# A float32 Hymba-style decoder block on one core: the last pass's rows fetched ahead of a scatter, the end of the program in another order, the first loads on two queues, and unread products in TensorE's waits

## The reference, cut to what matters

```python
h = _rmsnorm(x, norm1_g)
z = h @ w_in                      # u_ssm | q | 6 k/v parts | gates
y_ssm = _s5_mixer(u_ssm, ...)     # 32 groups of 16 channels, 64 complex states, scan over tokens, GELU, GLU
y_attn = _nsa_mixer(q, ...)       # compressed, selected and window attention, mixed by gates
x = x + concatenate([y_ssm, y_attn]) @ w_out
h = _rmsnorm(x, norm2_g)
x = x + _hier_moe(h, ...)         # 4 groups of 8 experts; top-1 group, top-2 experts in it, gated MLP of width 256
return _rmsnorm(x, final_g)
```

## Time and profile before

| | |
|---|---|
| median of 3 runs | 1100.4 us |
| the profiled execution | 1097.68 us |
| its span | 1095.8 us |
| granted TensorE clock, mean | 0.956 |
| PE busy | 1001.9 us (91%) |
| DVE busy | 487.8 us (45%) |
| ACT busy | 279.9 us (26%) |
| POOL busy | 152.5 us (14%) |

### The profile page before, as it was taken

One profiled execution on the slowest core, in us unless ns is written; L12 is line 12 of the kernel. 1 busy time (PEld: TensorE's weight loads), 2 busy tenths in 40 slices (PEclk: granted clock), 3 DMA queues, 4 the chain that ended last, 5 costly groups with the idle time before them and its releaser, 6 DMA issues. The chain is left out here.

```text
span 1095.8 us, 13448 instructions
## 1 busy us (share of the span) xinstructions
PE 1001.9 (91%) x5091; PEld 588.6 (54%) x5091; DVE 487.8 (45%) x1212; ACT 279.9 (26%) x630; POOL 152.5 (14%) x147
## 2 busy tenths in 40 slices
PE   6999999986799999999999999996999889899882
PEld 4434677765565466766667455564454334444431
DVE  3477661049635456665665224264732111112115
ACT  3200011130222376666655011020101000001133
POOL 4000000032201221211010000011121111211231
PEclk9999999997899989999999999996999989999986
DMA  9201020042500190000000232546789999999964
GB/s 258 99 1 45 1 77 1 1 44 78 97 1 0 33 280 3 1 1 2 1 2 1 77 144 106 211 159 240 290 308 352 366 410 396 394 390 385 348 201 172
DMA packets 53345, 163.70 MB, mean 149 GB/s; under 512 B 24347, under 2 KB 26459, under 8 KB 40919
## 3 DMA queue, kind: packets, MB, share of 16 engines
q1 hardware_dynamic: 45184, 144.42, 36.4%
q0 software_dynamic: 8096, 18.42, 6.6%
HBM read 145.31 MB, written 25.24 MB: 156 GB/s over the span
## 5 line engine op out<-in xcount | busy, mean ns | idle before, releaser
L1932 PE MATMUL banks<-shared,wout 128*64 128x512 f32 (+1 forms) x416 | 148.9, 624 | 10.3 <-issue 8.6
L1540 PE MATMUL banks<-wout,shared 128*128 128x512 f32 x256 | 112.7, 594 | 0.5 <-PEq L1200 0.5
L368 PE MATMUL banks<-x,wout 128*128 128x512 f32 x256 | 112.0, 594 | 1.1 <-DVE x L409 1.1
L1932 PEld LDWEIGHTS banks<-shared,wout 128*64 128x64 f32 (+1 forms) x416 | 56.8, 168 | 83.0 <-issue 82.6
L1248 ACT ACTIVATE shared<-shared,low 128x640 f32<-128x640 f32 (+7 forms) x128 | 92.9, 729 | 3.0 <-DVE low L1335 2.5
L1980 DVE SCALAR_TENSOR_TENSOR mix_bt<-mix_bt,slot_coef,banks 128x256 f32<-128x256 f32 x24 | 11.5, 480 | 171.1 <-ACT mix_bt L1960 171.1
L1298 PE MATMUL banks<-consts,shared 128*128 128x128 f32 x528 | 79.2, 286 | 1.9 <-ACT shared L1248 1.1
L1954 PE MATMUL banks<-shared,hidt 128*64 128x512 f32 (+1 forms) x208 | 75.3, 611 | 5.9 <-issue 4.6
L368 PEld LDWEIGHTS banks<-x,wout 128*128 128x128 f32 x256 | 47.8, 190 | 60.2 <-issue 58.1
L1298 PEld LDWEIGHTS banks<-consts,shared 128*128 128x128 f32 x528 | 56.9, 142 | 41.6 <-issue 36.7
L1540 PEld LDWEIGHTS banks<-wout,shared 128*128 128x128 f32 x256 | 47.6, 190 | 55.2 <-issue 55.2
(11 more groups left out here) (362 smaller groups left out, 1264.9 us busy)
## 6 DMA issues: line engine op xcount, KB each, us to landing
shared<-in_exp_w_down SPq DMA_DIRECT2D x26, 1024.0 KB, 18.2
shared<-in_exp_w_gate SPq DMA_DIRECT2D x26, 1024.0 KB, 16.9
shared<-in_exp_w_up SPq DMA_DIRECT2D x26, 1024.0 KB, 21.5
x<-in_exp_w_gate SPq DMA_DIRECT2D x6, 1024.0 KB, 15.6
x<-in_exp_w_up SPq DMA_DIRECT2D x6, 1024.0 KB, 23.2
x<-in_exp_w_down SPq DMA_DIRECT2D x6, 1024.0 KB, 24.2
shared<-in_x SPq DMA_DIRECT2D x8, 512.0 KB, 7.7
wout<-in_w_in SPq DMA_DIRECT2D x2, 2048.0 KB, 8.4
```

The lines of the kernel that those rows point to most:

```text
L368: ins = nc.tensor.matmul(bank[:], slot[:, c, c0:c0 + P], ht[:, c, half * 512:half * 512 + 512], **flags)
L1540: ins = nc.tensor.matmul(psum[n % 4], src[:, i * P:i * P + P], m["wout"][:, k, half * 512:half * 512 + 512], start=k == 0, stop=k == KD - 1)
L1932: ins = nc.tensor.matmul(psum[2 + p][rows].rearrange("p (a f) -> p a f", a=2), xt[:, p, k, rows], wgu[b][:, :, k], start=k == 0, stop=k == ...
```

## The change

The first loads: x's tile 0 and the gain are issued by ACT, each on a semaphore of its own, the constants and tiles 1 to 3 by SP. PE and ACT wait for tile 0 alone, then for tile 1. A new helper, `keep_warm`, issues products of the identity with 512 columns of the constants into a bank that nobody reads: 7 ahead of the wait for m3, 7, 14 and 6 among the waits of the state-space stage, and 11 ahead of the wait for pass 0's rows. In the state-space stage the wait for `products` moves from the third round to the second, and `own(4)` to `own(7)` are spread over rounds 1 to 3. At the end, gather 23 moves ahead of a scatter, and ACT's, DVE's and SP's lists take another order; tiles 0 and 1 are now the shared ones.

```diff
@@ stage_project
+    def x_landed(eng, i):
+        if i < 2:
+            eng.wait_ge(x_in[0] if i else x_first, 16)
+        else:
+            eng.wait_ge(x_in[i // 2], 32)
...
-            sp.dma_start(x_tile[0], x_view[0]).then_inc(x_in[0], 16)
             sp.dma_start(m["consts"][:], d["consts"]).then_inc(consts_in, 16)
-            sp.dma_start(g1[:], d["norm1_g"][0].rearrange("(p k) -> p k", k=KD)).then_inc(consts_in, 16)
-            for i in range(1, 4):
-                sp.dma_start(x_tile[i], x_view[i]).then_inc(x_in[i // 2], 16)
+            sp.dma_start(x_tile[1], x_view[1]).then_inc(x_in[0], 16)
+            for i in (2, 3):
+                sp.dma_start(x_tile[i], x_view[i]).then_inc(x_in[1], 16)
...
+            act.dma_start(x_tile[0], x_view[0]).then_inc(x_first, 16)
+            act.dma_start(g1[:], d["norm1_g"][0].rearrange("(p k) -> p k", k=KD)).then_inc(g_in, 16)
             for i in range(4):
                 square(i)
...
@@ stage_s5
+            keep_warm(nc, m, psum[0], 7)
             pe.wait_ge(m3_in, 16 * 2 * STEPS)
...
             for n in range(4):
-                if n == 2:
+                if n == 1:
                     pe.wait_ge(products, 16)
-                    for later in range(4, 8):
-                        own(later)
+                    own(4)
+                    own(5)
+                    keep_warm(nc, m, psum[7], 7)
+                elif n == 2:
+                    own(6)
+                    keep_warm(nc, m, psum[7], 14)
+                elif n == 3:
+                    keep_warm(nc, m, psum[7], 6)
+                    own(7)
                 pe.wait_ge(turned, n + 1)
...
+def keep_warm(nc, m, bank, count):
+
+    for _ in range(count):
+        nc.tensor.matmul(bank, m["ident"], m["consts"][:, 0:512], start=True, stop=True)
...
@@ stage_moe
-    by_norm = [("x", i) for i in (0, 1, 5, 6, 7)] + [("z", i) for i in range(DIRECT)]
-    shared_tiles = (2, 3, 4)
-    store_order = (0, 1, 2, 5, 3, 6, 4, 7)
+    by_norm = [("x", i) for i in range(2, NT)] + [("z", i) for i in range(DIRECT)]
+    shared_tiles = (0, 1)
+    store_order = (2, 3, 4, 0, 5, 1, 6, 7)
...
-                    gp.wait_ge(s["x_t"], 2 * (n + 2 - UN) + 2)
-                    gather(n + 2)
+                    for ahead in ((n + 2, n + 3) if n + 4 == NP else (n + 2,) if n + 4 < NP else ()):
+                        gp.wait_ge(s["x_t"], 2 * (ahead - UN) + 2)
+                        gather(ahead)
...
             act_gate(act, first, first % 2)
-            squares((0, 1, 2, 3))
+            squares((0,))
             act_gate(act, first + 1, (first + 1) % 2)
             act_hid(act, first, first % 2)
+            squares((1, 2, 3))
+            act_hid(act, first + 1, (first + 1) % 2)
             act_roots(act, groups[0], 4)
-            squares((4, 5))
-            act_hid(act, first + 1, (first + 1) % 2)
-            squares((6, 7))
+            squares((4, 5, 6, 7))
             act_roots(act, groups[1], 8)
-            scaled_tile(2, ("x", 0))
             squares((8, 9))
             act_roots(act, groups[2], 10)
-            scaled_tile(3, ("x", 0))
-            scaled_tile(4, ("x", 5))
+            for i in shared_tiles:
+                scaled_tile(i, ("x", 2))
...
+            keep_warm(nc, m, psum[7], 11)
             pe.wait_ge(x_in[0], 16)
...
             dve.wait_ge(fg_in, 16)
+            dve_sum(dve, first)
             inverses(0)
-            dve_scaled(("x", 0))
-            dve_sum(dve, first)
-            dve_scaled(("x", 1))
+            for i in (2, 3):
+                dve_scaled(("x", i))
+            dve_sum(dve, first + 1)
             inverses(1)
-            dve_sum(dve, first + 1)
-            for i in (5, 6, 7):
+            for i in (4, 5, 6, 7):
                 dve_scaled(("x", i))
             inverses(2)
```

More of the change, by code:

```diff
@@ L194, in stage_project @@
     count = {kind: [sum(job[0] == kind for job in jobs[:k + 1]) for k in range(len(jobs))] for kind in "ft"}
+    x_first, g_in = sem("x_first_in"), sem("norm1_g_in")
+    def x_landed(eng, i):
[3 more added lines that the diff above has]
+            eng.wait_ge(x_in[i // 2], 32)
     with nc.Block() as block:
@@ L245, in square @@
             def square(i):
-                act.wait_ge(x_in[i // 2], 32)
+                x_landed(act, i)
                 if i >= 2:
@@ L258, in scale_row @@
                 nc.scalar.copy(scale[:, h * 512:h * 512 + 512], psum[3]).then_inc(scale_out, 1)
+            act.dma_start(x_tile[0], x_view[0]).then_inc(x_first, 16)
+            act.dma_start(g1[:], d["norm1_g"][0].rearrange("(p k) -> p k", k=KD)).then_inc(g_in, 16)
             for i in range(4):
                 square(i)
-            act.wait_ge(consts_in, 32)
+            act.wait_ge(consts_in, 16)
             roots(0)
@@ L305, in x_transposes @@
             def x_transposes(i):
-                pe.wait_ge(x_in[i // 2], 32)
+                x_landed(pe, i)
                 for half in range(2):
@@ L375, in job @@
                 ins.then_inc(mm_done, 1)
-            pe.wait_ge(consts_in, 32)
+            pe.wait_ge(consts_in, 16)
             for i in range(4):
@@ L434, in _ @@
             V.memset(tabx[BUCKETS:BUCKETS + 1], MASKED).then_inc(masked_in, 1)
-            dve.wait_ge(consts_in, 32)
+            dve.wait_ge(consts_in, 16)
+            dve.wait_ge(g_in, 16)
             for i in range(4):
@@ L1848, in stage_moe @@
     junk = m["first_rows"][:].rearrange("p b i q -> p b (i q)")
-    last_in = [(t, 48) for t in m["tiles_in"]] + [(t, 16 * n + 16) for t, n in zip(m["x_stored"] + m["xn_stored"][:1], (4, 2, 2, 4))]
+    last_in = [(t, 48 if k else 32) for k, t in enumerate(m["tiles_in"])] + [(t, 16 * n + 16) for t, n in zip(m["x_stored"] + m["xn_stored"][:1], (4, 2, 2, 4))]
     ss_done, root_done, o_done, out_stored = sem("ss3_done"), sem("root3_done"), sem("o_done3"), sem("out_stored")
```

## The result

The changed kernel takes 1110.37 us (median of 4, 1108.55 to 1111.11), the kernel before, timed beside it, 1100.4 (its three undisturbed runs; a fourth took 1495.32 and is left out): a ratio of 1.0091, 95% interval 1.0073 to 1.011. It is slower by about 10 us, 0.9%. The prediction had 1109.5, in a range of 1103 to 1115. The profiled execution is 1108.55 us with a span of 1106.6; against the span of before, 1095.8, that is +10.8.

A forecast was written before the change was run, and what follows sets the result against it. The prediction took PE's list as the bound, with DVE setting the state-space stage until the fill lengthens PE's list. Terms -1.2 + 15.9 + 3.2 - 8.8 = +9.1 gave 1109.5 us against the median, range 1103 to 1115.

The forecast's parts named there:

- The price of an unread product: All fill batches: one unread product shows as two entries of 0.43 us, so costs 0.86 us at full clock.
- State-space stage, +15.9: State-space stage: fill lengthens PE's list, round 3 ends 17.4 us later, transposes gain 1.5; +15.9 us, bounds +14 to +18.
- Router to first pass, +3.2: Ahead of pass 0: eleven unread products end 5.9 us behind the rows' landing, part given back by faster work; +3.2 us.
- some 4 us in: Eleven unread products ahead of pass 0: the clock rises some 4 us into the batch, which ends at 759.9.
- near 762: Sign to look for: the first gate-and-up product starts near 762, at the full clock.
- some 7 us in, +6: Upper bound of the router-to-first-pass term: were the clock to rise some 7 us in, it would be +6 us.
- Start, -1.2: Kernel start: tile 0 goes at once, so job(0) starts at 14.5 instead of 15.78; -1.2 us, none to -2.5.
- about 0.5 on PE and 4 x 0.62 on DVE: Kernel start: time the four halves of tiles 2 and 3 need after landing at about 11.5, before job(0).
- End, -8.8: Kernel end: earlier gather 23 gives 4.6 us, ACT's and DVE's reordered lists the rest; -8.8 us, least 4.6, most 11.
- Half price: Rival: an unread product costs one entry, 0.43 us; sum -7.3 us, 1093 us; chance 0.06.
- The clock pays: Rival: fill hides in waits DVE and DMAs set anyway and cold work shrinks; sum -16 us, 1084.5 us; chance 0.05.
- The end gives only its wait: Rival: the end gains only -4.6 us, stores or reading back holding the rest; sum +13.3, 1113.7 us; chance 0.12.

The follow-up runs named there:

- old_start: The changed kernel with the first loads as before the change (tile 0 and the gain on SP's queue): 1109.74 us, ratio 1.009 to the kernel before.
- gather_only: The kernel before with one edit, gather 23 issued behind gather 22, ahead of scatter 19: 1093.69 us, ratio 0.9927.
- fitted_fill: The changed kernel with unread products recounted and placed to fit the waits, 3 of them ahead of the first pass: 1085.12 us, ratio 0.9872 to the kernel before.
- end_lists_only: The kernel before with only the new end lists of ACT, DVE and SP; gather 23 stays behind scatter 19: 1095.3 us, ratio 0.9934.
- no_fill: The changed kernel without any unread product, its order of rounds, start and end kept: 1089.82 us, ratio 0.9914 to the kernel before.
- no_fill_old_rounds: no_fill with the state-space rounds also as before the change, leaving only the new start and end: 1089.66 us, ratio 0.9911 to the kernel before.

## Why the prediction was right, point by point

The mechanism was right: PE's list became the bound of the state-space stage, and its excess outweighed a gain at the end that was nearly as forecast. The sum came out closer than its terms. On the spans +9.1 met +10.8; the start and the router's stretch were 1.5 and 1.2 us too good, the stage and the end 0.4 and 0.7 too bad, and that these partly cancel is luck.

- *The price of an unread product.* Right: 14 entries in 6.12 us is 0.87 us a product, from the one row of a twin.
- *State-space stage, +15.9.* Measured +15.5. The walk through PE's list was right row by row: round 3 was to end at 301.4 and ended at 301.5, the transposes were to take 4.0 and took 3.89. The clock rose at about 271, where 270.9 was taken. Window of the changed kernel (us, PE busy, PEclk, DMA share, GB/s):

```profile
271.00:272.00 1.00, 1.00 (x3) 0.99 0.00 0
```

  The kernel without unread products has the same order of rounds and takes 2.1 us less than before here, so the term is theirs, and the order adds nothing to it.
- *Router to first pass, +3.2.* Measured +4.4. The step that was mis-sized is the moment of the rise, "some 4 us in": the batch began at 763.90 and the rise came at about 769.4, 5.5 in, so 12.3 us of fill where 11.4 was written. The same view:

```profile
769.00:770.00 1.00, 1.00 (x3) 0.82 0.54 131
```

  So the transposes began 6.6 us later behind the list products than before, for 5.9; less was given back, too, 0.7 for 1.0 ahead of the gate-and-up products and 1.6 for 1.8 in them. In old_start, which has the same eleven, they took 11.4 us and the term was +3.2 (24.55 for 21.31): the miss is of the size of the spread between runs. The sign "near 762" for the first gate-and-up product leaves out the shift of the earlier stages; less the 15.46 us by which the list products were late, it came at 762.75. The bound "some 7 us in, +6" is a slip: by the same sum it is +4.7.
- *Start, -1.2.* Wrong: +0.3, and nothing that two pairs of kernels could tell. The step that failed is "about 0.5 on PE and 4 x 0.62 on DVE" behind tile 3's landing. The landing itself (11.70) was as taken, but the 16 transposes that followed it took 3.56 us, 0.22 each, near the pace of the half clock, so PE set the rate and not DVE's 0.62 a half; in the kernel without unread products the same 16 took 2.65 and the first product came at 15.41. The gain g1 landed at 9.4, which the prediction did not see either; it cost nothing here: DVE ended the first four halves at 12.07 and then waited 0.79 us for PE.
- *End, -8.8.* Measured -9.5. The list was right row by row. Less the 20.31 us by which the axis was late, the first root ended at 1061.9, where 1061.8 was written, and the last scaled tile at 1072.55, where 1072.8 was; the last 0.5 us were won behind that tile. Both mechanisms are shown apart, in the traces. The gather alone was worth 5.4, not 4.6. Half of the 0.8 missing is the down product behind pass 23's transposes, 3.67 us here where it began at the half clock before and took 4.11, which the prediction left out. Timeline of PE, gather_only:

```profile
1038.56 1.06 PE L1923 MATMUL banks<-consts,wout 128*128 128x128 f32 x8
1039.49 3.67 PE L1954 MATMUL banks<-x,hidt 128*128 128x512 f32 x8
```

- *The rivals.* Half price: no, by the row of 14 entries. The clock pays: not here, as PE had no wait left to hide the fill in; the mechanism is real where the fill fits its wait (-4.5 us in fitted_fill). The end gives only its wait: no, end_lists_only gains with the wait still there.
- *The rule of the Trainium skill* ("TensorE: Matmul & The Clock Gate", Part 1, the cold stretch priced at half its time) roughly fits round 3, which took 2.06 for 3.78. What it does not price, the fill itself, cost 20.6 us in the change, net of what the clock gave back; cut to the waits, fill and clock together gained some 4.5.

## What to carry to other kernels

Price a filler instruction from a row of the same shape and type before choosing its count; a float32 product shows as two entries, and to count a product at one of them makes every batch twice as long as planned. Fill a wait only up to the instant its releaser comes, and put the batch where the bank is already free, or the fill becomes the bound. A change that helps (here some 10 us, at the end) can hide behind one that costs twice as much, so time the parts apart.

## What the runs showed of the hardware that was not expected

- The same code of the state-space stage took 65.20, 66.56, 66.86 and 67.80 us in four kernels that do not differ in it, with the 32 transposes at 3.90, 5.54, 5.95 and 5.96. The one-microsecond windows show why: in the shortest the clock fell and rose three times from 260 on, and was back at 1.00 when the transposes began at 285.61; in the longest it was at 0.50 from 281 until 291. When the clock falls and rises within a stage of many short waits differs from run to run.
- At the start the windows give a granted clock of 1.00, but the first eight transposes, from 5.94, took 1.94 us, 0.24 each, the pace of the half clock (1.97 for eight in the earlier trace rows). In no_fill 7 transposes ran in the microsecond from 12 and 10 in the next, with the column at 1.00 in both. In these first microseconds the column does not show the pace.
- The landing of the sixteen small DMAs of m3 moves, too: PE could go on at 249.45 in the kernel before and at 248.43 in no_fill_old_rounds, whose stages have the same code and began at 225.65 and 225.74.
